# The opening of a two-block transformer kernel: VectorE takes over part of the weight split, and x's later quarters are transposed inside units

## The chip, the cores and the metric

One core of one Trainium2 chip runs one launch of the kernel. The metric is the device time in microseconds; less is better. Weights, activations and output are in DRAM in float32 at the start and at the end.

## The reference, cut to what matters

The kernel computes two transformer blocks on a sequence of 256 rows of 1024 columns. The change touches only the first step of the first block, the product of the normed input with `w_in`:

```python
def rms_norm(x, g):
    x32 = x.astype(jnp.float32)
    y = x32 * lax.rsqrt(jnp.mean(jnp.square(x32), axis=-1, keepdims=True) + RMS_EPS)
    return (y * g.astype(jnp.float32)).astype(x.dtype)

# first block: two attentions on slices of z, gated and merged, an MLP, a gated embedding
u = rms_norm(h, g_mix[i])          # (1, 256, 1024)
z = u @ w_in[i]                    # w_in: (1024, 4360)
q_a, k_a, v_a, q_b, k_b, v_b, f_b, gate_logits = jnp.split(z, SPLIT_POINTS, axis=-1)
```

The second block (sparse attention, retention, a gated MLP) follows with its own weights.

## The kernel before, in words

**Products in three parts.** TensorE multiplies in the type float32r, which keeps fewer bits than float32. So each operand is split: the upper half is its copy in float32r (`w_hi`, `xT_hi`), the lower half what is left (`w_lo`, `xT_lo`), and a product is the sum of upper x upper, upper x lower and lower x upper. ScalarE makes the upper halves with a copy, VectorE the lower ones with a subtraction.

**Units.** Weights come in units: two contraction tiles of 128 rows by 512 columns, 512 KB, one load on SP's queue into one of eight slots of `raw`; the split goes into one of four slots of `w_hi` and `w_lo`. A unit costs TensorE 12 products of 512 columns: two contraction tiles (`kk`), two tiles of 128 sequence rows (`t`), three parts. Units 0 to 3 make the first 512 columns of z (the queries), units 4 to 7 the next 512, and so on, until the last weights of the second block. The semaphores `hi_done`, `lo_done` and `units_used` count units split above, split below and used up. The root mean square is not applied in front: x times `g_mix` is multiplied, and the rows are scaled afterwards.

**The input.** x arrives in quarters of 256 columns (`load_x`, two loads of 128 KB each, semaphores `x_q0` to `x_q3`) into `h`. TensorE transposes them against the identity into banks of PSUM (`transposes`, four instructions a quarter, L1852). ScalarE copies a bank with `g_mix` as scale to `xT_hi` (`wide_hi`, L589: two operations, then one count of `wt_hi`), VectorE makes `xT_lo` from bank and copy (`wide_lo`, L1048, then one count of `wt_lo`). Unit `kp` of the first chunk needs the quarter `kp`. The first quarter is taken tile by tile (L639 on ScalarE, L1135 on VectorE).

**The order of the opening** is written out by hand, for each engine.
- SP (L424 to L433): first quarter of x; unit 0 in two loads of 256 KB (`first_in` and `landed[0]`); second quarter; unit 1 in one load; third quarter; unit 2; last quarter; units 3 to 7.
- GpSimd (L489): after a small constant it clears the padded arrays of keys and values, four instructions on Z, and then waits for the first norm.
- TensorE (L1892 to L1956): six products of ones by ones as filler (`ones_products`, L1890); transpose of `g_mix`; transposes of x's first quarter; two more fillers; unit 0's first contraction tile (six products, L1943, L1946, L1949); transposes of the second quarter; unit 0's second tile; transposes of the third quarter; unit 1 (L1920, L1924, L1927); transposes of the last quarter; units 2 and 3 (`unit_pair_lows_last`, L1734, L1743, L1746); then the usual units (`unit_pair`, L1709 to L1711).
- ScalarE (L634 to L660): `g_mix`; x's first tile (L639); the first tile of unit 0 (L643); x's second tile; unit 0's second tile (L646); the second quarter of x; unit 1 in two operations (L651); the third quarter of x; units 2 and 3 (`split_to`, L569); the last quarter; unit 4; sums of squares of x (L605); unit 5; and so on.
- VectorE (L1126 to L1151): four clearings and constants, `ones` the last; lower halves of x and unit 0, tile by tile (L1135, L1138); second quarter; unit 1 (L1145); third quarter; units 2 and 3 (L1032); last quarter; units 4 and 5.

An engine works through its instructions in order, and a wait holds all that stand behind it.

Of the kernel before, what the change touches and what calls it, by code (L numbers as in the profile page):

```python
# [7 lines left out]
P = 128  # L8
F32 = mybir.dt.float32
F32R = mybir.dt.float32r  # L10
BF16 = mybir.dt.bfloat16
ALU = mybir.AluOpType
# [47 lines left out]
def constants():  # L60
# [33 lines left out]
    "ident_in": "identity", "first_in": "first contraction tile of the first unit", "first_hi": "ACT: its upper half", "first_lo": "DVE: its lower half", "consts_in": "the other constants", "x_q0": "x, first quarter of the columns", "x_q1": "x, second quarter", "x_q2": "x, third quarter of its columns", "x_q3": "x, the last",  # L94
    "second_hi": "ACT: upper half of the second unit's first contraction tile", "second_lo": "DVE: its lower half",
# [76 lines left out]
def build(nc, x, p, g_mix, w_in, b_forget, swa_sinks, w_br_swa, w_br_fox, w_mix_out, g_mlp, w_ff1, w_ff2,  # L172
# [87 lines left out]
    with ExitStack() as ctx:  # L260
# [5 lines left out]
        def sem(name):  # L266
            return sems[name]
# [144 lines left out]
        def _(sp):  # L412
# [15 lines left out]
            load(1)  # L428
# [129 lines left out]
        def _(act):  # L558
# [78 lines left out]
            for kk, (bank, x_half) in enumerate(((2, sem("x_hi")), (6, sem("wt_hi")))):  # L637
                act.wait_ge((sem("x_T"), sem("wt_done"))[kk], 1)
                nc.scalar.activation(xT_hi[:, kk, :], B[:, bank, 0:SEQ], ACT.Copy,  # L639
                                     scale=vec[:, V_GMIX + kk:V_GMIX + kk + 1]).then_inc(x_half, 1)  # L640
                if kk == 0:
                    act.wait_ge(sem("first_in"), 16)
                    nc.scalar.activation(w_hi[:, 0, 0, :], raw[:, 0, 0, :], ACT.Copy).then_inc(sem("first_hi"), 1)  # L643
# [6 lines left out]
            for kk, upper_half in enumerate((sem("second_hi"), hi_done)):  # L650
                nc.scalar.activation(w_hi[:, 1, kk, :], raw[:, st.slot[1], kk, :], ACT.Copy).then_inc(upper_half, 1)  # L651
# [365 lines left out]
        def _(dve):  # L1017
# [107 lines left out]

            nc.vector.memset(one_row[:, :], 0.0).then_inc(sem("zeros"), 1)  # L1126
# [3 lines left out]
            nc.vector.memset(ones, 1.0).then_inc(sem("ones"), 1)  # L1130
            dve.wait_ge(sem("vec_done"), 1)
            for kk, (x_upper, x_lower, upper_half, lower_half) in enumerate(((sem("x_hi"), sem("x_lo"), sem("first_hi"), sem("first_lo")),
                                                                             (sem("wt_hi"), sem("wt_lo"), hi_done, lo_done))):
                dve.wait_ge(x_upper, 1)
                nc.vector.scalar_tensor_tensor(xT_lo[:, kk, :], B[:, (2, 6)[kk], 0:SEQ], vec[:, V_GMIX + kk:V_GMIX + kk + 1],  # L1135
                                               xT_hi[:, kk, :].bitcast(F32), ALU.mult, ALU.subtract).then_inc(x_lower, 1)
                dve.wait_ge(upper_half, 1)
                nc.vector.tensor_tensor(w_lo[:, 0, kk, :], raw[:, 0, kk, :], w_hi[:, 0, kk, :].bitcast(F32),  # L1138
                                        ALU.subtract).then_inc(lower_half, 1)
            wt[0] = 1  # L1140
            done[0] = 1
            wide_lo((3,), xT_hi, xT_lo, 2, V_GMIX)
            for kk, (upper_half, lower_half) in enumerate(((sem("second_hi"), sem("second_lo")), (hi_done, lo_done))):
                dve.wait_ge(upper_half, 1 + kk)
                nc.vector.tensor_tensor(w_lo[:, 1, kk, :], raw[:, st.slot[1], kk, :], w_hi[:, 1, kk, :].bitcast(F32),  # L1145
                                        ALU.subtract).then_inc(lower_half, 1)
# [559 lines left out]
        def _(pe):  # L1706
# [20 lines left out]

            def unit_pair_lows_last(u, xh, xl, kt0, banks, last):
# [3 lines left out]
                for kk in range(2):  # L1732
                    for t in range(TILES):
                        nc.tensor.matmul(B[:, banks[t], :], xh[:, kt0 + kk, rows_of(t)], w_hi[:, s, kk, :], start=False, stop=False)  # L1734
                for lows in ("weights", "rows") if last else ("rows", "weights"):
# [150 lines left out]

            def ones_products(n):
# [12 lines left out]
            ones_products(2)  # L1900
            for c in range(5):
                banks = (2 * (c % 2), 2 * (c % 2) + 1)
                for kp in range(4):
# [12 lines left out]
                    if u == 1:  # L1916
                        for kk, (upper_half, lower_half) in enumerate(((sem("second_hi"), sem("second_lo")), (hi_done, lo_done))):
                            pe.wait_ge(upper_half, 1 + kk)
                            for t in range(TILES):
                                nc.tensor.matmul(B[:, banks[t], :], xT_hi[:, 2 + kk, rows_of(t)], w_hi[:, 1, kk, :], start=False, stop=False)  # L1920
                            if kk == 0:
                                pe.wait_ge(sem("wt_lo"), 2)
                            for t in range(TILES):
                                nc.tensor.matmul(B[:, banks[t], :], xT_lo[:, 2 + kk, rows_of(t)], w_hi[:, 1, kk, :], start=False, stop=False)  # L1924
                            pe.wait_ge(lower_half, 1 + kk)
                            for t in range(TILES):
                                m = nc.tensor.matmul(B[:, banks[t], :], xT_hi[:, 2 + kk, rows_of(t)], w_lo[:, 1, kk, :], start=False, stop=False)  # L1927
                        m.then_inc(units_used, 1)
# [8 lines left out]
                    else:  # L1937
                        for kk, (x_upper, upper_half, x_lower, lower_half) in enumerate((
                                (sem("x_hi"), sem("first_hi"), sem("x_lo"), sem("first_lo")), (sem("wt_hi"), hi_done, sem("wt_lo"), lo_done))):
                            pe.wait_ge(x_upper, 1)  # L1940
                            pe.wait_ge(upper_half, 1)
                            for t in range(TILES):
                                nc.tensor.matmul(B[:, banks[t], :], xT_hi[:, kk, rows_of(t)], w_hi[:, 0, kk, :], start=kk == 0, stop=False)  # L1943
                            pe.wait_ge(x_lower, 1)
                            for t in range(TILES):
                                nc.tensor.matmul(B[:, banks[t], :], xT_lo[:, kk, rows_of(t)], w_hi[:, 0, kk, :], start=False, stop=False)  # L1946
                            pe.wait_ge(lower_half, 1)
                            for t in range(TILES):
                                m = nc.tensor.matmul(B[:, banks[t], :], xT_hi[:, kk, rows_of(t)], w_lo[:, 0, kk, :], start=False, stop=False)  # L1949
                            if kk == 0:  # L1950
                                pe.wait_ge(sem("x_q1"), 32)
                                transposes((3,), lambda t, k: h[:, t, (2 + k) * P:(3 + k) * P], "wt_done")
                        m.then_inc(units_used, 1)
                    if u < 2:
                        pe.wait_ge(sem(("x_q2", "x_q3")[u]), 32)
                        transposes((4 + u,), lambda t, k: h[:, t, (4 + 2 * u + k) * P:(5 + 2 * u + k) * P], "wt_done")  # L1956
# [388 lines left out]
```

## Time and profile before

| | |
|---|---|
| Runs without a profile | 824.35, 824.30, 824.13 us; median 824.3 |
| The profiled execution's own time | 823.81 us |
| Its span, first to last instruction | 822.1 us |
| Mean granted TensorE clock in the span | 0.998 |
| Busy: TensorE, its weight loads, VectorE, ScalarE, GpSimd | 812.8, 677.7, 629.3, 462.9, 61.9 us |
| Read from DRAM over the span | 170.42 MB |

The profile is of one execution. Its times in the rows count from the first instruction of the span; an engine's busy time is the union of its instructions' spans, and matmuls overlap, so that the end of one in the timeline lies behind the start of the next. The chain of waits is followed back from the last instruction, at each step to what released it or to the instruction before it on its engine; its pieces don't overlap, and a piece of TensorE there ends where its last product ends. In the timeline consecutive instructions of one kind are one row: start, us from the first start to the last end, engine, line, operation, out<-in, shapes, count, and in brackets the idle time before it with what ended it. PE is TensorE, PEld its weight loads, DVE VectorE, ACT ScalarE, POOL GpSimd.

### The profile page before, as it was taken

How to read it: one execution, taken by the hardware profiler on the slowest of the kernel's cores; microseconds unless marked ns; L12 is line 12 of the kernel's file. 1: busy time of each engine (PE TensorE's matmuls, PEld its weight loads, DVE VectorE, ACT ScalarE, POOL GpSimd, SP SyncE). 2: the span in 40 equal slices, each digit the busy share in tenths (PEclk: the TensorE clock that was granted, in tenths of full speed). 3: DMA queues.
4: the chain of work that ended last, by engine and by line, in shares of the span. 5: the costliest groups of instructions: out<-in, count | busy, mean ns of one | idle time of the engine just before them, and what ended most of it. 6: DMA issues, size and time to landing. Idle time of an engine off the chain costs nothing.

```text
span 822.1 us, 12294 instructions
## 1 busy us (share of the span) xinstructions
PE 812.8 (99%) x4272; PEld 677.7 (82%) x4272; DVE 629.3 (77%) x965; ACT 462.9 (56%) x751; POOL 61.9 (8%) x89
## 2 busy tenths in 40 slices
PE   9999999999999999999999999999999999999996
PEld 7897777898888888877978877888888888888885
DVE  5567777687888898878878997456796877677776
ACT  6657765466555555568544466446346654455444
POOL 2100000110011110301510000010000000000000
PEclk9999999999999999999999999999999999999999
DMA  9867435779999999543965574555544666655641
GB/s 302 275 198 237 136 126 182 251 273 405 346 335 340 319 323 336 191 120 106 272 213 143 164 218 137 171 154 153 180 154 128 201 189 209 196 178 172 209 130 52
DMA packets 89213, 173.15 MB, mean 211 GB/s; under 512 B 6553, under 2 KB 37001, under 8 KB 89041
## 3 DMA queue, kind: packets, MB, share of 16 engines
q1 hardware_dynamic: 83008, 142.56, 54.2%
q0 software_dynamic: 6000, 29.93, 10.5%
q8 instruction: 27, 0.44, 0.2%
q14 instruction: 18, 0.14, 0.0%
q10 hardware_dynamic: 160, 0.07, 0.0%
HBM read 170.42 MB, written 1.06 MB: 209 GB/s over the span
## 4 chain that ended last, share of the span: by engine, by line
PE 95%; DVE 2%; issue 1%; ACT 1%; POOLq 0%; POOL 0%; ACTq 0%; DVEq 0%
PE B L1709 19%; PE B L1711 19%; PE B L1710 19%; PE B L1772 15%; PE B L1775 8%; PE B L1852 2%; PE B L1787 2%; PE B L1882 2%; PE B L1860 1%; PE B L1873 1%; PE B L2126 1%; PE B L1790 1%; DVE w_lo L1032 1%; PE B L1818 0%; PE B L1809 0%
## 5 line engine op out<-in xcount | busy, mean ns | idle before, releaser
L1032 DVE TENSOR_TENSOR w_lo<-raw,w_hi 128x1024 fp32r<-128x1024 f32 (+3 forms) x154 | 184.8, 1209 | 49.4 <-ACT w_hi L569 47.9
L1709 PE MATMUL B<-w_hi,xT 128*128 128x512 f32 (+3 forms) x536 | 209.5, 391 | 0.0
L569 ACT ACTIVATE w_hi<-raw 128x1024 fp32r<-128x1024 f32 (+3 forms) x154 | 157.5, 1030 | 88.6 <-PE B L1711 74.6
L1711 PE MATMUL B<-w_hi,xT 128*128 128x512 f32 (+3 forms) x536 | 204.5, 381 | 0.0
L1710 PE MATMUL B<-w_lo,xT 128*128 128x512 f32 (+3 forms) x536 | 204.1, 381 | 0.0
L1709 PEld LDWEIGHTS B<-w_hi,xT 128*128 128x128 f32 x536 | 100.8, 188 | 20.7 <-issue 2.2
L1711 PEld LDWEIGHTS B<-w_hi,xT 128*128 128x128 f32 x536 | 100.7, 188 | 19.8
L1710 PEld LDWEIGHTS B<-w_lo,xT 128*128 128x128 f32 x536 | 100.9, 188 | 17.4
L1772 PE MATMUL B<-xT,w_hi 128*128 128x512 f32 x320 | 100.5, 395 | 0.0
L982 ACT ACTIVATE w_hi<-raw 128x1024 fp32r<-128x1024 f32 x60 | 62.2, 1055 | 42.5 <-PE B L1775 30.9
L1302 DVE TENSOR_TENSOR w_lo<-raw,w_hi 128x1024 fp32r<-128x1024 f32 x56 | 67.2, 1221 | 21.7 <-ACT w_hi L787 20.8
L1709 PE MATMUL B<-w_hi,sT 128*128 128x512 f32 (+1 forms) x201 | 78.9, 393 | 0.0
L1638 DVE TENSOR_TENSOR w_lo<-raw,w_hi 128x1024 fp32r<-128x1024 f32 x60 | 72.5, 1220 | 7.6 <-ACT w_hi L982 7.6
L1710 PE MATMUL B<-w_lo,sT 128*128 128x512 f32 (+1 forms) x201 | 77.9, 388 | 0.0
L1711 PE MATMUL B<-w_hi,sT 128*128 128x512 f32 (+1 forms) x201 | 77.9, 387 | 0.0
L787 ACT ACTIVATE w_hi<-raw 128x1024 fp32r<-128x1024 f32 x56 | 57.5, 1053 | 35.0 <-PE B L1775 30.6
L1775 PEld LDWEIGHTS B<-xT,w_lo 128*128 128x128 f32 x320 | 60.1, 188 | 14.1
L1772 PE MATMUL B<-sT,w_hi 128*128 128x512 f32 x224 | 70.3, 395 | 0.0
L1775 PE MATMUL B<-xT,w_lo 128*128 128x256 f32 x320 | 62.9, 278 | 0.0
L1310 DVE SCALAR_TENSOR_TENSOR Z<-Z,small 128x1536 f32<-128x1536 f32 x28 | 50.8, 1813 | 0.0
L1775 PEld LDWEIGHTS B<-sT,w_lo 128*128 128x128 f32 x224 | 42.1, 188 | 9.9
L1772 PEld LDWEIGHTS B<-xT,w_hi 128*128 128x128 f32 x320 | 49.4, 189 | 0.9 <-DVE Z L1624 0.2
(270 smaller groups left out, 1071.4 us busy)
## 6 DMA issues: line engine op xcount, KB each, us to landing
raw<-in_w_in_dram SPq DMA_DIRECT2D x79, 512.0 KB, 3.9
raw<-in_w_ff_dram SPq DMA_DIRECT2D x64, 512.0 KB, 7.4
Z<-in_w_ada_dram POOLq DMA_DIRECT2D x32, 768.0 KB, 7.6
raw<-in_w_ffn_gate_dram SPq DMA_DIRECT2D x44, 256.0 KB, 3.4
raw<-in_w_ffn_up_dram SPq DMA_DIRECT2D x44, 256.0 KB, 4.1
raw<-in_w_ffn_down_dram SPq DMA_DIRECT2D x20, 512.0 KB, 4.3
raw<-in_w_mix_out_dram SPq DMA_DIRECT2D x8, 512.0 KB, 3.7
raw<-in_w_ple_gate_dram SPq DMA_DIRECT2D x8, 512.0 KB, 4.3
```

The source lines that it names most:

```text
L569: nc.scalar.activation(w_hi[:, u % SPLIT, :, 0:n], raw[:, st.slot[u], :, 0:n], ACT.Copy).then_inc(hi_done, 1)
L787: nc.scalar.activation(w_hi[:, u % SPLIT, :, :], raw[:, st.slot[u], :, :], ACT.Copy).then_inc(hi_done, 1)
L982: nc.scalar.activation(w_hi[:, u % SPLIT, :, :], raw[:, st.slot[u], :, :], ACT.Copy).then_inc(hi_done, 1)
L1032: nc.vector.tensor_tensor(w_lo[:, u % SPLIT, :, 0:n], raw[:, st.slot[u], :, 0:n], w_hi[:, u % SPLIT, :, 0:n].bitcast(F32), ALU.subtract).t ...
L1302: nc.vector.tensor_tensor(w_lo[:, u % SPLIT, :, :], raw[:, st.slot[u], :, :], w_hi[:, u % SPLIT, :, :].bitcast(F32), ALU.subtract).then_in ...
L1310: nc.vector.scalar_tensor_tensor(ada_acc[:, 1536 * q:1536 * (q + 1)], ada_raw[:, q, :], silu_now, ada_acc[:, 1536 * q:1536 * (q + 1)], ALU ...
L1638: nc.vector.tensor_tensor(w_lo[:, u % SPLIT, :, :], raw[:, st.slot[u], :, :], w_hi[:, u % SPLIT, :, :].bitcast(F32), ALU.subtract).then_in ...
L1709: nc.tensor.matmul(bank, xh, wh, start=start, stop=False)
L1710: nc.tensor.matmul(bank, xh, wl, start=False, stop=False)
L1711: return nc.tensor.matmul(bank, xl, wh, start=False, stop=stop)
L1772: nc.tensor.matmul(B[:, i, :], w_hi[:, s, kk, cols], x2[:, kt0 + kk, :, :].rearrange("p e n -> p (e n)"), start=first and kk == 0, stop=False)
L1775: m = nc.tensor.matmul(B[:, i, SEQ:2 * SEQ], w_lo[:, s, kk, cols], x2[:, kt0 + kk, 0, :], start=False, stop=last and kk == 1)
```

## The change

The change has five parts, all in the opening.
- SP loads unit 1 in two halves, `second_in` and `landed[1]`.
- VectorE makes the upper half of unit 0's first contraction tile and of unit 1's first contraction tile, with a copy (`tensor_copy`), and each lower half right behind it; ScalarE no longer does. VectorE sets `ones` first of its constants, and takes the lower halves of x's first two tiles before the lower half of unit 0's second tile.
- TensorE computes one filler product instead of two before unit 0.
- In units 0 and 1 the products stand in another order, the weights' lower half before x's lower half (`products`, two products a call).
- The transposes of x's second quarter stand before unit 0's last pair of products, those of the third quarter inside unit 1 behind its sixth product, those of the last quarter inside unit 2 behind its fourth. Before, they stood behind unit 0's sixth product, behind unit 0 and behind unit 1.

```diff
@@ sync @@
-            load(1)
+            for kk, name in enumerate((sem("second_in"), landed[1])):
+                sp.dma_start(raw[:, st.slot[1], kk, :], w_in1[(2 + kk) * P:(3 + kk) * P, 0:512]).then_inc(name, 16)
@@ scalar @@
-                if kk == 0:
-                    act.wait_ge(sem("first_in"), 16)
-                    nc.scalar.activation(w_hi[:, 0, 0, :], raw[:, 0, 0, :], ACT.Copy).then_inc(sem("first_hi"), 1)
...
-            for kk, upper_half in enumerate((sem("second_hi"), hi_done)):
-                nc.scalar.activation(w_hi[:, 1, kk, :], raw[:, st.slot[1], kk, :], ACT.Copy).then_inc(upper_half, 1)
+            nc.scalar.activation(w_hi[:, 1, 1, :], raw[:, st.slot[1], 1, :], ACT.Copy).then_inc(hi_done, 1)
@@ vector @@
+            nc.vector.memset(ones, 1.0).then_inc(sem("ones"), 1)
             nc.vector.memset(one_row[:, :], 0.0).then_inc(sem("zeros"), 1)
...
-            nc.vector.memset(ones, 1.0).then_inc(sem("ones"), 1)
+            def opening_lo(slot, kk, upper_half, count, lower_half):
+                dve.wait_ge(upper_half, count)
+                nc.vector.tensor_tensor(w_lo[:, slot, kk, :], raw[:, st.slot[slot], kk, :], w_hi[:, slot, kk, :].bitcast(F32),
+                                        ALU.subtract).then_inc(lower_half, 1)
+
+            dve.wait_ge(sem("first_in"), 16)
+            nc.vector.tensor_copy(w_hi[:, 0, 0, :], raw[:, 0, 0, :]).then_inc(sem("first_hi"), 1)
+            opening_lo(0, 0, sem("first_hi"), 1, sem("first_lo"))
             dve.wait_ge(sem("vec_done"), 1)
-            for kk, (x_upper, x_lower, upper_half, lower_half) in enumerate(((sem("x_hi"), sem("x_lo"), sem("first_hi"), sem("first_lo")),
-                                                                             (sem("wt_hi"), sem("wt_lo"), hi_done, lo_done))):
+            for kk, (x_upper, x_lower) in enumerate(((sem("x_hi"), sem("x_lo")), (sem("wt_hi"), sem("wt_lo")))):
                 dve.wait_ge(x_upper, 1)
                 nc.vector.scalar_tensor_tensor(xT_lo[:, kk, :], B[:, (2, 6)[kk], 0:SEQ], vec[:, V_GMIX + kk:V_GMIX + kk + 1],
                                                xT_hi[:, kk, :].bitcast(F32), ALU.mult, ALU.subtract).then_inc(x_lower, 1)
-                dve.wait_ge(upper_half, 1)
-                nc.vector.tensor_tensor(w_lo[:, 0, kk, :], raw[:, 0, kk, :], w_hi[:, 0, kk, :].bitcast(F32),
-                                        ALU.subtract).then_inc(lower_half, 1)
             wt[0] = 1
-            done[0] = 1
+            opening_lo(0, 1, hi_done, 1, lo_done)
+            dve.wait_ge(sem("second_in"), 16)
+            nc.vector.tensor_copy(w_hi[:, 1, 0, :], raw[:, st.slot[1], 0, :]).then_inc(sem("second_hi"), 1)
+            opening_lo(1, 0, sem("second_hi"), 1, sem("second_lo"))
             wide_lo((3,), xT_hi, xT_lo, 2, V_GMIX)
...
+            opening_lo(1, 1, hi_done, 2, lo_done)
@@ tensor @@
+            def opening_transposes(name, bank, k0):
+                pe.wait_ge(sem(name), 32)
+                transposes((bank,), lambda t, k: h[:, t, (k0 + k) * P:(k0 + k + 1) * P], "wt_done")
+
             def unit_pair_lows_last(u, xh, xl, kt0, banks, last):
...
+                if u == 2:
+                    opening_transposes("x_q3", 5, 6)
...
+            def products(banks, rows, k, w, slot, kk, first=False):
+                for t in range(TILES):
+                    m = nc.tensor.matmul(B[:, banks[t], :], rows[:, k, rows_of(t)], w[:, slot, kk, :], start=first, stop=False)
+                return m
...
-            ones_products(2)
+            ones_products(1)
...
                     if u == 1:
+                        pe.wait_ge(sem("second_hi"), 1)
+                        products(banks, xT_hi, 2, w_hi, 1, 0)
+                        pe.wait_ge(sem("second_lo"), 1)
+                        products(banks, xT_hi, 2, w_lo, 1, 0)
+                        pe.wait_ge(hi_done, 2)
+                        products(banks, xT_hi, 3, w_hi, 1, 1)
+                        opening_transposes("x_q2", 4, 4)
+                        pe.wait_ge(sem("wt_lo"), 2)
+                        products(banks, xT_lo, 2, w_hi, 1, 0)
+                        products(banks, xT_lo, 3, w_hi, 1, 1)
+                        pe.wait_ge(lo_done, 2)
+                        products(banks, xT_hi, 3, w_lo, 1, 1).then_inc(units_used, 1)
...
                     else:
+                        pe.wait_ge(sem("x_hi"), 1)
+                        pe.wait_ge(sem("first_hi"), 1)
+                        products(banks, xT_hi, 0, w_hi, 0, 0, True)
+                        pe.wait_ge(sem("first_lo"), 1)
+                        products(banks, xT_hi, 0, w_lo, 0, 0)
+                        pe.wait_ge(sem("x_lo"), 1)
+                        products(banks, xT_lo, 0, w_hi, 0, 0)
+                        pe.wait_ge(sem("wt_hi"), 1)
+                        pe.wait_ge(hi_done, 1)
+                        products(banks, xT_hi, 1, w_hi, 0, 1)
+                        pe.wait_ge(sem("wt_lo"), 1)
+                        products(banks, xT_lo, 1, w_hi, 0, 1)
+                        opening_transposes("x_q1", 3, 2)
+                        pe.wait_ge(lo_done, 1)
+                        products(banks, xT_hi, 1, w_lo, 0, 1).then_inc(units_used, 1)
```

The loops that these lines of TensorE replace are in the printed functions above. ScalarE's order is otherwise as it was: the third quarter's copies stand before the split of units 2 and 3.

## Rows read from the trace of the kernel before

**Rows 1.** The page, busy us of each engine (share of the span) and instructions.
```profile
PE 812.8 (99%) x4272; PEld 677.7 (82%) x4272; DVE 629.3 (77%) x965; ACT 462.9 (56%) x751; POOL 61.9 (8%) x89
```

**Rows 2.** Waits of TensorE over the whole span: us in total, times, longest.
```profile
PE B L1890 <- DVE ones_r L1130: 1.4, 1, 1.4
```

**Rows 3.** The chain of waits, 0 to 20 us: start, us, what.
```profile
1.44 2.93 PE B L1890 x6
...
5.72 0.85 PE B L1890 x2
6.57 0.66 PE B L1943 x2
...
8.15 0.44 PE B L1852 x4
...
9.98 0.44 PE B L1852 x4
...
13.20 0.44 PE B L1852 x4
13.64 0.93 PE B L1734 x4
...
16.40 0.91 PE B L1734 x4
...
18.21 0.91 PE B L1743 x4
```

**Rows 4.** The timeline around the first product: start, us, engine, line, operation.
```profile
5.39 0.47 ACT L639 ACTIVATE xT<-B,vec 128x256 fp32r<-128x256 f32 x1 [0.61 <-PE B L1852]
...
5.77 0.62 ACT L643 ACTIVATE w_hi<-raw 128x512 fp32r<-128x512 f32 x1
...
6.42 0.69 DVE L1138 TENSOR_TENSOR w_lo<-raw,w_hi 128x512 fp32r<-128x512 f32 x1
...
6.53 0.70 PE L1943 MATMUL B<-w_hi,xT 128*128 128x512 f32 x2
```

**Rows 5.** DMA issues at 1.81 and 3.70 us: xcount, KB each, us to landing.
```profile
raw<-in_w_in_dram SPq DMA_DIRECT2D x1, 256.0 KB, 3.5
...
raw<-in_w_in_dram SPq DMA_DIRECT2D x1, 512.0 KB, 5.3
```

**Rows 6.** VectorE groups by line and shape: busy us, mean ns, idle before.
```profile
L1385 DVE CAST xT<-Z 128x256 fp32r<-128x256 f32 x16 | 4.6, 289 | 2.6 <-ACT Z L860 2.6
L1111 DVE TENSOR_SCALAR Z<-Z,small 128x256 f32<-128x256 f32 x24 | 8.3, 348 | 0.0
L1111 DVE TENSOR_SCALAR Z<-Z,small 128x128 f32<-128x128 f32 x24 | 6.9, 287 | 0.8
```

**Rows 7.** The timeline of GpSimd at 5.3 us.
```profile
4.13 1.92 POOL L489 MEMSET Z<- 128x2176 f32 x1
```

**Rows 8.** The timeline of VectorE and GpSimd where they overlap, 179.5 and 380 us.
```profile
179.85 1.02 DVE L1269 TENSOR_SCALAR Z<-Z,small 128x1536 f32<-128x1536 f32 x1
...
180.02 1.42 POOL L484 TENSOR_TENSOR small<-small 128x2 f32<-128x2 f32 x1 [24.44 <-DVE small L1063]
...
380.21 0.54 POOL L530 TENSOR_TENSOR small<-small 128x1 f32<-128x1 f32 x1
...
380.26 0.29 DVE L1371 TENSOR_SCALAR rstd_id<-cst,small 128x128 f32<-128x128 f32 x1 [0.40 <-POOL small L484]
```

**Rows 9.** The timeline, from transposed quarters of x to ScalarE's copies.
```profile
7.99 0.60 PE L1852 MATMUL B<-cst,h 128*128 128x128 f32 x4
...
8.63 0.84 ACT L589 ACTIVATE xT<-B,vec 128x256 fp32r<-128x256 f32 x2 [1.36 <-PE B L1852]
...
9.36 1.15 ACT L651 ACTIVATE w_hi<-raw 128x512 fp32r<-128x512 f32 x2
...
11.19 1.06 ACT L569 ACTIVATE w_hi<-raw 128x1024 fp32r<-128x1024 f32 x1
```

**Rows 10.** The timeline, VectorE's split of the sixth unit.
```profile
18.63 1.22 DVE L1032 TENSOR_TENSOR w_lo<-raw,w_hi 128x1024 fp32r<-128x1024 f32 x1 [0.84 <-ACT w_hi L569]
```

More of the change, by code:

```diff
@@ L92 @@
 SIGNALS = {
-    "ident_in": "identity", "first_in": "first contraction tile of the first unit", "first_hi": "ACT: its upper half", "first_lo": "DVE: its lower half", "consts_in": "the other constants", "x_q0": "x, first quarter of the columns", "x_q1": "x, second quarter", "x_q2": "x, third quarter of its columns", "x_q3": "x, the last",
-    "second_hi": "ACT: upper half of the second unit's first contraction tile", "second_lo": "DVE: its lower half",
+    "ident_in": "identity", "first_in": "first contraction tile of the first unit", "first_hi": "DVE: its upper half", "first_lo": "DVE: its lower half", "consts_in": "the other constants", "x_q0": "x, first quarter of the columns", "x_q1": "x, second quarter", "x_q2": "x, third quarter of its columns", "x_q3": "x, the last",
+    "second_in": "first contraction tile of the second unit", "second_hi": "DVE: upper half of the second unit's first contraction tile", "second_lo": "DVE: its lower half",
     "x_T": "PE: x's first contraction tile transposed", "x_hi": "ACT: upper half of x's first contraction tile", "x_lo": "DVE: its lower half",
@@ L1136, in _ @@
                                                xT_hi[:, kk, :].bitcast(F32), ALU.mult, ALU.subtract).then_inc(x_lower, 1)
-                dve.wait_ge(upper_half, 1)
-                nc.vector.tensor_tensor(w_lo[:, 0, kk, :], raw[:, 0, kk, :], w_hi[:, 0, kk, :].bitcast(F32),
-                                        ALU.subtract).then_inc(lower_half, 1)
             wt[0] = 1
-            done[0] = 1
+            opening_lo(0, 1, hi_done, 1, lo_done)
+            dve.wait_ge(sem("second_in"), 16)
+            nc.vector.tensor_copy(w_hi[:, 1, 0, :], raw[:, st.slot[1], 0, :]).then_inc(sem("second_hi"), 1)
+            opening_lo(1, 0, sem("second_hi"), 1, sem("second_lo"))
             wide_lo((3,), xT_hi, xT_lo, 2, V_GMIX)
[L1143 to L1146, printed above, removed]
+            opening_lo(1, 1, hi_done, 2, lo_done)
             done[0] = 2
@@ L1916, in _ @@
                     if u == 1:
[L1917 to L1928, printed above, removed]
+                        pe.wait_ge(sem("second_hi"), 1)
[10 more added lines that the diff above has]
+                        products(banks, xT_hi, 3, w_lo, 1, 1).then_inc(units_used, 1)
                     elif u in (2, 3):
@@ L1937, in _ @@
                     else:
[L1938 to L1956, printed above, removed]
+                        pe.wait_ge(sem("x_hi"), 1)
+                        pe.wait_ge(sem("first_hi"), 1)
+                        products(banks, xT_hi, 0, w_hi, 0, 0, True)
+                        pe.wait_ge(sem("first_lo"), 1)
```

## The prediction

> **What bounds the kernel now.** I read the page first: TensorE is busy for 812.8 of 822.1 us [rows 1], so only time in which it stands still, or filler that it computes, can be won. The view of waits then asks what TensorE waits for: one entry, 1.4 us before its very first instruction [rows 2]. Everything else stands in the chain of waits, in order of time, which in the opening runs over TensorE alone [rows 3]. The reader is to see that its pieces touch: filler ends at 6.57 us, the first pair of products at 7.23, the transposes of x's second quarter at 8.59, of the third at 10.42, unit 1 at 13.20, the transposes of the last quarter at 13.64, then unit 2 to 16.40 and unit 3 to 19.12. Four products take 0.91 us, 0.23 each; four transposes 0.44. From 6.57 us on there is no gap to remove. What the change can win is the start, and what it can lose is this density.
>
> A second thing is in the same rows: the two filler products took 0.43 us each (0.85 for two), those after 6.57 us 0.23. These are the two levels of the clock, 1.2 and 2.4 GHz; TensorE had been at work since 1.44 us when it rose, near 6.4 us.
>
> **What sets the start.** The timeline around the first product [rows 4]: ScalarE makes x's upper half until 5.39 + 0.47 = 5.86, then the weights' upper half until 5.77 + 0.62 = 6.39, and the first product starts at 6.53, 0.14 after that. The pair ends at 6.53 + 0.70 = 7.23. The change gives that weight half to VectorE. Its weights land at 1.81 + 3.5 = 5.3 us [rows 5].
>
> **Cost of the cast on VectorE.** The trace has casts of 256 columns, both sides in SBUF, at 289 ns; TENSOR_SCALAR takes 287 ns for 128 columns and 348 for 256 [rows 6], so 0.48 ns a column. 512 columns are then 289 + 256 x 0.48 = 412 ns, taken as 0.42 us. Bounds: 0.29 (256 columns) and 0.69 (a VectorE subtraction of 512, rows 4). Nothing in its way, the cast ends at 5.3 + 0.1 + 0.42 = 5.8, x's half at 5.86 decides, and the first product starts at 6.0: 0.5 us won. The clock takes part of it back, since until about 6.4 a product takes 0.43: the second starts at about 6.47 and the pair ends at 6.86, 0.37 before today's 7.23.
>
> **The port.** Something is in its way. GpSimd clears 2176 columns from 4.13 to 6.05 us in one instruction [rows 7]. Where VectorE runs a fast one-input instruction, the trace shows GpSimd held: a TENSOR_SCALAR of 1536 columns runs 179.85 to 180.87, and GpSimd's little power operation of 180.02 takes 1.42 us instead of 0.54 [rows 8], so that it ends 0.57 after the other. So one keeps the other out for a whole instruction. Here the order is the reverse, GpSimd first. The nearest row for that, a TENSOR_SCALAR at 380.26 begun 0.05 us into a GpSimd operation, shows nothing (0.29 us, as in rows 6), but that operation touches one column and can hold little. Between a wait of 0 and one until 6.05 I take the latter: the clearing writes throughout its 1.92 us. The cast then ends at 6.05 + 0.42 = 6.47 and the first product starts at 6.61, 0.08 later than now.
> The Trainium skill, "SBUF — State Buffer", section "Who interferes with whom", has the rule: VectorE in a two-port mode (copy and cast among its operations) and GpSimd share a port pair, and whoever issues first holds it for the whole instruction. By that rule the sum is the +1.94 below, without it +1.23; the trace agrees for the order VectorE first, and no row shows the other.
>
> **Unit 0.** The subtraction follows the cast: 6.50 + 0.69 = 7.19 [rows 4], so the third product starts at 7.33 instead of 7.07 and its pair ends at 8.03. Three pairs follow (lower half of x, then the second tile's two): 3 x 0.46, to 9.41. Their inputs are in time: VectorE makes x's two lower halves from 7.19 on, at most 0.69 each as a bound, so by 7.88 and 8.57, wanted at 8.03 and 8.95; the second upper half of the weights comes no later than today, since ScalarE has one operation less in front. Then the transposes of x's second quarter, moved from behind six products to behind ten: 9.85. That x has landed by then, since they run at 7.99 today [rows 9]. Behind them unit 0 has one pair left, 0.46.
>
> **Gap 1.** Unit 1 needs the columns transposed just now. ScalarE starts 0.04 after the transposes (7.99 + 0.60 = 8.59, start 8.63), its two copies take 0.84 [rows 9], the product follows 0.14 after, and a pair that starts on an idle array takes 0.70: 9.85 + 0.04 + 0.84 + 0.14 + 0.70 = 11.57 for the end of unit 1's first pair. Unhindered it were 9.85 + 2 x 0.46 = 10.77: a gap of 0.80. Today the same copies lie behind the second half of unit 0 and the third quarter's transposes (8.59 to 10.42).
>
> **Gap 2.** Two more pairs, to 12.49, then the third quarter's transposes, to 12.93, and three pairs as cover (1.38). ScalarE's queue, though, is in order: its two copies for that quarter, and only behind them the split of unit 2. Today the split runs at 11.19 with 1.06 us, long before 13.64. In the new order it starts 0.04 + 0.73 (8.63 to 9.36) after the transposes and ends, 1.06 later, at 14.76; the first pair of unit 2 ends at 14.76 + 0.14 + 0.70 = 15.60 against 14.77 unhindered: a gap of 0.83. Then a pair (16.06), the last quarter's transposes, now inside unit 2 (16.50), and four pairs: unit 2 ends at 18.34. Today: 16.40. The sum is +1.94.
>
> **Afterwards.** Unit 3's rows are copied by 16.50 + 0.88 = 17.4, before 18.34: no third gap. VectorE finished unit 5's split at 18.63 + 1.22 = 19.85 [rows 10] and TensorE needs it at 19.12 + 2.73 = 21.85; it moves with the rest, so 2 us of cover stay. The work removed, one filler product, is worth nothing: it filled a wait. The earlier filler, at the front, neither. One more DMA issue on SP costs 0.47 us of its queue (1.81 to 3.70 us is four issues, rows 5); x's later quarters and unit 2 are wanted later than today by more than that. Unit 1 lands whole at 3.70 + 5.3 = 9.0 today [rows 5], its first half so no later; VectorE is busy with unit 0 until at most 8.57 + 0.69 = 9.26, cast and subtraction of the half take it to 10.37, and TensorE wants them at 10.9 and 11.57. That cast finds GpSimd done with its clearing [rows 7]. The rest of the program is dense and its loads are freed by TensorE's progress, so I pass the delay on in full.
>
> **Sum.** Against the profiled execution, 823.8 us with a span of 822.1: 825.8. The median of the runs is 824.3, 0.5 above: 824.3 + 1.94 = **826.2 us**. A measurement tells about 0.2%, 1.65 us, from no change, so the line lies at 825.95: close, and the port decides on which side.
>
> **Rivals.**
> - No port wait, chance 0.25. First pair at 6.86, four pairs to 8.70, transposes 9.14, then the same two gaps: unit 2 ends at 17.63, +1.23, 825.5. For it speaks the row at 380.26; against it the one at 180.02. If the port pushes the transposes out by over 0.42 us (I have 0.71), the total passes 1.65.
> - The clock rises late, 0.10. It rose near 6.4 us, with TensorE at work since 1.44 almost without pause. In the new kernel it stands still from about 5.8 to 6.6. If it stays low through unit 0, twelve products cost 0.20 more each, 2.4 us: 828.6. Against it: today's pauses around the little transposes (4.37 to 5.3) did no harm.
> - Not slower, 0.07: the gaps do not open, because x's copies are ready within the one pair that follows the transposes. The place is unit 1's first product; it decides at 0.46 us after the transposes. The price is then that of the start alone: -0.37 without the port's wait, 823.9; +0.34 with it (8.03 for today's 7.69), 824.6. Against it: 0.04 + 0.84 + 0.14 are 1.02, of rows without a wait in them.
>
> **How the numbers follow.** The forecast has 0.55, and within it 0.1 for gaps small enough to stay under 1.65; 0.03 is for what I don't see. Slower 0.56 = 0.45 + 0.10 for the late clock + 0.01; same 0.42 = 0.25 + 0.10 + 0.07; faster 0.02. The forecast alone is 825.8 to 826.8 (cast 0.29 to 0.69, 0.15 either way on each gap); the range 825.0 to 827.3 takes in the rival without a wait and leaves out the late clock and the start alone.
>
> **What would show it.** In the new profile: the cast's end, 6.5 (port) or 5.8; the first product at 6.6 or 6.0; two waits of TensorE, on ScalarE's copy of x before unit 1 and on ScalarE's split of unit 2, some 0.7 to 0.8 us each in the spacing of products; a spacing of 0.23 from 6.6 on; unit 2's end at 18.34 and everything behind it 2 us late. Wrong it is if unit 1's first product starts before 10.3 with port wait, if unit 2 starts without a pause, or if a later stage takes the delay back.

## The result and the profile after

The changed kernel takes **825.48 us** (median of 11 runs, 825.34 to 826.87) against 824.10 for the kernel before beside it (11 runs, 823.66 to 824.35): ratio 1.0020, 95% interval 1.0012 to 1.0027. By the medians that is 1.38 us or 0.17% slower: inside the range of the prediction (825.0 to 827.3), but near its fast end, below the 825.8 to 826.8 that it gave for its own mechanism, and just under the 0.2% that it called distinguishable. The profiled execution took 825.48 us with a span of 823.7; the one of before 823.81 with 822.1.

The page (busy us, share, instructions) shows that TensorE does the same work and that the span is 1.6 us longer:

```profile
span 823.7 us, 12293 instructions
...
PE 813.2 (99%) x4271; PEld 677.3 (82%) x4271; DVE 631.1 (77%) x967; ACT 462.3 (56%) x749; POOL 61.8 (7%) x89
```

Where before there was one wait of TensorE [rows 2], the view of waits now has four (us in total, times, longest):

```profile
PE B L1906 <- DVE ones_r L1123: 1.2, 1, 1.2
PE B L1742 <- ACT w_hi L570: 0.6, 1, 0.6
PE B L1900 <- DVE w_hi L1136: 0.6, 1, 0.6
PE B L1900 <- ACT xT L590: 0.5, 1, 0.5
```

The three new ones are the three places of the prediction: VectorE's cast in front of unit 0 (L1136), ScalarE's copy of x in front of unit 1 (L590), ScalarE's split in front of unit 2 (L570). The chain of waits (start, us, what) puts them in order; it left TensorE nowhere in this stretch before [rows 3]:

```profile
5.05 1.29 DVE w_hi L1136
...
6.47 2.73 PE B L1900 x10
9.20 0.45 PE B L1862 x4
...
9.68 0.85 ACT xT L590 x2
10.53 0.04 issue
10.57 1.65 PE B L1900 x6
12.22 0.45 PE B L1862 x4
...
12.70 0.84 ACT xT L590 x2
13.54 0.96 ACT w_hi L570
14.49 0.14 issue
14.63 1.16 PE B L1742 x4
15.79 0.44 PE B L1862 x4
...
18.06 0.91 PE B L1742 x4
```

The reader is to see: the cast until 6.33; ten products, then the second quarter's transposes until 9.65; TensorE released only after both copies of x (9.68 to 10.53); six products and the third quarter's transposes until 12.68; then not only the copies but, behind them in ScalarE's queue, the split of unit 2 (13.54 to 14.49); the last quarter's transposes inside unit 2. Unit 2 ends at 18.06, where it ended at 16.40 [rows 3]: +1.66. The whole profiled execution is 1.67 longer. Nothing after unit 2 gave any of it back, and nothing added to it. The 1.66 are made up of 0.12 up to the end of the second quarter's transposes (9.65, where ten products and four transposes ended at 9.53 before), 0.73 for the pause before unit 1 and 0.82 for the one before unit 2; these are differences of the rows, rounded.

The timeline around the start (start, us, engine, line, operation, shapes, count), to be held against [rows 4, 7]:

```profile
4.13 1.92 POOL L490 MEMSET Z<- 128x2176 f32 x1
...
5.05 1.27 DVE L1136 CAST w_hi<-raw 128x512 fp32r<-128x512 f32 x1 [3.66 <-DMA raw<-in_w_in_dram]
6.36 0.69 DVE L1132 TENSOR_TENSOR w_lo<-raw,w_hi 128x512 fp32r<-128x512 f32 x1
...
8.35 0.42 DVE L1146 CAST w_hi<-raw 128x512 fp32r<-128x512 f32 x1
...
7.11 0.73 PE L1900 MATMUL B<-w_lo,xT 128*128 128x512 f32 x2
...
10.57 0.73 PE L1900 MATMUL B<-w_hi,xT 128*128 128x512 f32 x2 [0.46 <-ACT xT L590]
```

The clearing runs from 4.13 to 6.05 as before. The cast begins at 5.05 and takes 1.27; its twin for unit 1, at 8.35 with GpSimd idle, takes 0.42.

In six of the variants below the clearing also stands whole before the cast. The chains of two of them (first the one with all transposes at their old places, then the one with the second quarter put back) show the cast beginning at other moments, as its weights land:

```profile
5.00 1.34 DVE w_hi L1136
```

```profile
5.25 1.08 DVE w_hi L1136
```

Both end at 6.33 or 6.34. In all seven profiles with the whole clearing the cast begins between 5.00 and 5.28 and ends at 6.32 to 6.34: its end is tied to the clearing's, not to its own start.

### The profile page after: what moved, and what is told of

The parts are those of the page before. It is cut to its first block, busy times and chain, and to the rows that moved or that the text cites. A ratio compares the mean times of both kernels' runs of the same rounds, so it can differ in the third digit from the quotient of the medians.

```text
span 823.7 us, 12293 instructions
## 1 busy us (share of the span) xinstructions
PE 813.2 (99%) x4271; PEld 677.3 (82%) x4271; DVE 631.1 (77%) x967; ACT 462.3 (56%) x749; POOL 61.8 (7%) x89
## 3 DMA queue, kind: packets, MB, share of 16 engines
HBM read 170.42 MB, written 1.06 MB: 208 GB/s over the span
## 4 chain that ended last, share of the span: by engine, by line
PE 97%; ACT 0%; DVE 0%; DMA 0%; issue 0%; SPq 0%; POOLq 0%; POOL 0%; ACTq 0%; DVEq 0%
PE B L1712 20%; PE B L1714 20%; PE B L1713 20%; PE B L1782 15%; PE B L1785 8%; PE B L1862 2%; PE B L1797 2%; PE B L1892 2%; PE B L1870 1%; PE B L1883 1%; PE B L2138 1%; PE B L1800 1%; PE B L1900 1%; PE B L1828 0%; PE B L1819 0%; PE B L1830 0%
## 5 line engine op out<-in xcount | busy, mean ns | idle before, releaser
L570 ACT ACTIVATE w_hi<-raw 128x1024 fp32r<-128x1024 f32 (+3 forms) x154 | 157.4, 1030 | 87.7 <-PE B L1714 74.7
```

The lines of the kernel that those rows point to most:

```text
L570: nc.scalar.activation(w_hi[:, u % SPLIT, :, 0:n], raw[:, st.slot[u], :, 0:n], ACT.Copy).then_inc(hi_done, 1)
```

## The experiments

Each kernel is the changed one with the edit shown, unless said otherwise, and was run 11 times (one of them 9), with the kernel before beside it. One thing must be known to read the times: many of the kernels fall into two groups of runs whose means lie 1.4 to 1.7 us apart, and the profiles show what differs (below, the clock). Where it matters the lower groups are compared; that leaves out how many runs fall into the upper one, which changes from kernel to kernel and can put the median there.

**The port set free.**

```diff
@@ gpsimd @@
+            pool.wait_ge(sem("first_hi"), 1)
             zero(vb_pad[:, :, :])
```

> The changed kernel, but GpSimd starts its last clearing only after VectorE's cast of the first weights. Theory (the cast of 1.28 us is 0.42 of work and 0.86 of waiting for GpSimd's clearing of 4.13 to 6.04): the cast takes 0.42 and ends by 5.6, x's upper half decides (5.64), TensorE's first product starts at 5.8 instead of 6.47, and with the lower clock taking some of it back the time falls by 0.4 to 0.65 us, 825.5 to about 824.9. Rival (this cast is slow by itself, on freshly landed data or in this type): the cast stays near 1.28 and the time stays at 825.5.

Measured: 824.87 us (824.61 to 825.22), five runs at 824.61 to 824.66. The cast, in the timeline, and two pieces of the chain of waits, from an execution of 825.20:

```profile
5.15 0.43 DVE L1137 CAST w_hi<-raw 128x512 fp32r<-128x512 f32 x1 [3.76 <-DMA raw<-in_w_in_dram]
```

```profile
5.80 3.21 PE B L1901 x10
...
14.43 1.16 PE B L1743 x4
```

The cast takes 0.43 us: the waiting for GpSimd's clearing is shown, the rival is out. TensorE starts on this execution at 5.8 (of ten products those at the front take 0.43 each: 3.21 us for ten against 2.73 in the changed kernel), so part of the 0.7 won goes to the clock. The pauses before units 1 and 2 are still there, and in this execution, one of the slower of the 11, unit 2 starts only 0.2 earlier (14.43 for 14.63). The five quickest runs are 0.8 below the 825.4 of the changed kernel's main group.

**The clearing cut in two.**

```diff
@@ gpsimd @@
-            zero(vb_pad[:, :, :])
+            nc.gpsimd.memset(vb_pad[:, 0, :], 0.0)
+            zero(vb_pad[:, 1, :])
```

> The changed kernel, but GpSimd clears the last array in two instructions of 1088 columns instead of one of 2176. Nobody waits for anybody new. Theory (the port is held for one instruction and no longer): the first half ends at about 5.1, VectorE's cast of 5.05 starts behind it and ends by 5.6, the second half is held up in its turn, TensorE starts at 5.8, and the runs whose clock rises early come to 824.65 as in the run with the port free. Rival (GpSimd keeps the port as long as it has clearings queued): the cast ends at 6.3 as in the changed kernel, 825.4.

Measured: 825.52 (824.48 to 827.22). The timeline of GpSimd and of VectorE:

```profile
4.12 1.00 POOL L496 MEMSET Z<- 128x1088 f32 x1
5.07 1.00 POOL L490 MEMSET Z<- 128x1088 f32 x1
...
5.12 1.24 DVE L1137 CAST w_hi<-raw 128x512 fp32r<-128x512 f32 x1 [3.73 <-DMA raw<-in_w_in_dram]
```

The profile doesn't separate the two theories. The second half began at 5.07, the cast at 5.12, 0.05 later, and it ended at 6.36, behind the end of that half (6.07). So a lead of 0.05 us was enough for GpSimd to keep the cast out to the end of its instruction; that it does so only for one instruction, and not for as long as clearings are queued, isn't shown, since this was the last one. The profile and the main group of runs (five at 825.46 to 825.54) came out as the rival said. For the theory speak two of the 11 runs, 824.48 and 824.61, the time of the kernel with the port free: that the cast was first in them is likely, but they carry no profile.

**ScalarE splits unit 2 first.**

```diff
@@ scalar @@
+            split_to(2)
             wide_hi((4,), xT_hi, 4, V_GMIX)
             split_to(3)
```

> The changed kernel, but ScalarE splits unit 2 before it copies x's third quarter. Theory (gap 2 comes from ScalarE's order): TensorE starts unit 2 at 13.9 instead of 14.63, -0.7 us, 824.8. Rival (unit 2's weights are what is late: they landed at 11.8): a pause before unit 2 stays, now released by the DMA, and less than 0.3 is won.

Measured: median 825.93, with four runs at 824.66 to 824.71, one at 825.00 and six at 825.93 to 826.44. The profiled execution (826.44) is of the upper group; its ScalarE timeline and its waits of TensorE show what the edit does:

```profile
11.44 0.84 ACT L590 ACTIVATE xT<-B,vec 128x256 fp32r<-128x256 f32 x2 [4.77 <-PE B L1863]
...
12.68 1.06 ACT L570 ACTIVATE w_hi<-raw 128x1024 fp32r<-128x1024 f32 x1
14.46 0.84 ACT L590 ACTIVATE xT<-B,vec 128x256 fp32r<-128x256 f32 x2 [0.72 <-PE B L1863]
```

```profile
PE B L1901 <- ACT xT L590: 0.5, 1, 0.5
PE B L1901 <- DVE w_hi L1137: 0.4, 1, 0.4
```

The split of unit 2 (12.68) now stands before the copies of the third quarter (14.46), and the wait for it is gone from the view. In this execution everything came over 1.5 us later, so it can't tell whether unit 2's weights would be late in the lower group; the times can: the four runs at 824.7 are 0.7 under the changed kernel's 825.4. Gap 2 came from the order on ScalarE, at the size expected. The median is still above the changed kernel's, since more runs fell into the upper group.

**The second quarter's transposes back behind the sixth product.**

```diff
@@ tensor @@
                         products(banks, xT_lo, 0, w_hi, 0, 0)
+                        opening_transposes("x_q1", 3, 2)
...
                         products(banks, xT_lo, 1, w_hi, 0, 1)
-                        opening_transposes("x_q1", 3, 2)
```

> The changed kernel, but x's second quarter is transposed behind unit 0's sixth product, as before the change. Theory (gap 1 comes from the place of these four transposes): no pause before unit 1, its first product at 10.0 instead of 10.57, and gap 2 keeps its size, so -0.55 us, 824.9. Rival (x's second quarter or unit 1 lands too late to use the earlier place): a pause before the transposes takes its place, and the time stays within 0.2 of 825.5.

Measured: 824.74, with six runs at 824.65 to 824.74 and five at 826.07 to 826.50. The chain of waits of the profiled execution (826.50, upper group):

```profile
6.47 2.90 PE B L1900 x6
9.37 0.85 PE B L1862 x4
10.22 3.09 PE B L1900 x12
13.31 0.45 PE B L1862 x4
...
15.71 1.16 PE B L1742 x4
```

Twelve products of units 0 and 1 follow each other without a pause between the units: gap 1 is gone, gap 2 (until 15.71) is not. That is seen at the slower product rate, which gives x's copies more cover, but the times agree: in the lower group 0.7 is won. Expected was 0.55, which counted only the later start of unit 1; the pair that starts behind the pause also takes 0.73 (10.57 to 11.30) instead of 0.46.

**All transposes at their old places.** The edit just shown, and:

```diff
@@ tensor @@
-                if u == 2:
-                    opening_transposes("x_q3", 5, 6)
...
-                        opening_transposes("x_q2", 4, 4)
...
+                    if u < 2:
+                        opening_transposes(("x_q2", "x_q3")[u], 4 + u, 4 + 2 * u)
```

> The changed kernel with all of x's transposes at their places of before; left of the change are VectorE's casts, unit 1 in two loads, one filler less and the order of the products. Theory: no pause before units 1 and 2; only the port's wait and the third product's wait for the subtraction are left, TensorE 0.15 behind the kernel before at the sixth product and at unit 3, so 824.05 to 824.3 for runs whose clock rises early. Rival (the extra load or the order of the products costs something by itself): over 824.6 in these runs.

Measured: median 825.24, but four runs at 823.90 to 824.00 and seven at 825.17 to 825.76. In the waits of TensorE in the profiled execution (825.65, upper group), beside the one before its first instruction, this is all:

```profile
PE B L1898 <- DVE w_hi L1136: 0.7, 1, 0.7
```

Only the cast's wait is left. In the lower group the time is 823.95, 1.45 under the changed kernel, and about that of the kernel before: the casts, the extra load and the new order of the products together cost next to nothing here (0.1 less than expected). The moved transposes cost nearly all of the slowdown of the lower group, and the two gaps taken away one by one (0.7 each) add up to it. The upper group, though, is now most of the runs, and the median is 1.2 above the kernel before.

**The filler, and the clock.** One filler more, two more, none:

```diff
@@ tensor @@
-            ones_products(1)
+            ones_products(2)
```

> The changed kernel with two filler products in front of unit 0, as before the change, instead of one; TensorE waits there until 6.33 anyhow. The runs so far fall in two groups, 1.4 to 1.6 us apart, and in the profiles of the slower group the clock rises at 10.7 or 10.8 us instead of 5.8. Theory (the standstill before unit 0 decides how often it rises late): the time of the faster group stays at 825.4, and 0 or 1 run in 11 is in the slower group. Rival (it is independent of the filler): 2 to 6 of 11.

> The changed kernel with three filler products in front of unit 0, so that TensorE works until about 6.45, as long as it waits for the cast. Theory (the standstill in front of unit 0 lets the clock rise late): none of 11 runs in the slower group, as in the kernel before, where no run of 64 lay 1.4 us above the rest but one; the time stays at 825.4 to 825.6. Rival (something else in the new opening does it): 2 or more of 11 at 826.8 to 827.2.

> The changed kernel with no filler product in front of unit 0. Theory (the standstill decides): most of the 11 runs, 7 or more, are in the slower group, and the median is about 826.9. Rival (independent of the filler): 2 to 6 of 11, and the median mostly at 825.5.

Measured: with two, 825.51, eight runs at 825.42 to 825.54 and three at 826.99 to 827.11. With three, 825.45, and none of 11 runs above 825.92. With none, 826.94: four of nine at 825.36 to 825.49, five at 826.94 to 827.27. The changed kernel with its one filler: nine at 825.34 to 825.54, two at 826.82 and 826.87. None of the edits moves the lower group; what differs is how many runs lie in the upper. And in the other direction, on the kernel before:

```diff
@@ tensor, the kernel before @@
-            ones_products(2)
+            ones_products(1)
```

> The kernel before with one filler product instead of two in front of unit 0; its first product still waits for ScalarE until 6.5. Theory (the standstill): 2 to 6 of 11 runs come out 1.2 to 1.7 us above the rest, at about 825.2 to 825.6, the rest at 823.6 to 824.4. Rival: no such run, 824.0 as before.

Measured: 823.77, nine runs at 823.57 to 824.30 and two at 825.40 and 825.73. The profiled one took 825.73; its chain of waits (pieces of two products, the first also with the start):

```profile
6.43 1.19 PE B L1943 x2
7.62 0.85 PE B L1946 x2
...
10.18 0.85 PE B L1943 x2
11.04 0.55 PE B L1946 x2
11.58 0.46 PE B L1949 x2
```

A pair of products takes 0.85 us, 0.43 each, until about 11.1, and 0.46 from then on: by the duration of the products the clock stayed at 1.2 GHz for two thirds of unit 0, where in the kernel before it had risen by 6.57 [rows 3]. The profile of the kernel with the second quarter put back (826.50) shows the same above, 0.85 us for its first four transposes where they take 0.44 otherwise, and the chain of the profiled execution without filler (827.06) has ten slow products in front of the second quarter's transposes, against 2.73 us in the changed kernel:

```profile
6.47 4.39 PE B L1900 x10
```

The level is read from durations alone: the granted clock that the profiles give is 1.00 in every stretch between 4.5 and 12 us, in both groups.

Taken alone, 0 of 11 with three fillers against 2 of 11 with one proves little, and so does 2 of 11 for the kernel before with one filler, against 2 of 97 with its own two. But the other kernels can be sorted in the same way, each against kernels run beside it on the same chip:

- Without a standstill, the port free (the first experiment and the version with the third quarter inside unit 1, below): 1 of 22 runs in an upper group. Beside them, with the cast's wait (ScalarE's split first, the second quarter back): 11 of 22.
- With the cast's wait (the clearing cut, two fillers, none, all old places): 19 of 42. Beside them, the kernel before: 0 of 31.
- Without a standstill or with one of 0.2 us (three fillers, and the two versions below in their last runs): 0 of 33.

So that a standstill in front of unit 0 goes with the upper group is shown. Its size is not: two fillers leave a wait of 0.3 us for the cast by the view of waits (one leaves 0.6, none 1.0, three no such entry), and still gave 3 of 11, where 0 or 1 was expected, and without filler it was 5 of 9, where 7 were. With one filler it was 2 of 11 in the changed kernel, but 6 of 11 with ScalarE's split moved, an edit that touches nothing before about 11 us, and 4, 5 and 7 of 11 in the other variants with one filler and the cast's wait. So 11 runs don't tell 0.3 from 1.0 us, and what length of standstill at which moment matters stays open.

**Versions with the port free and fewer pauses.** The kernel with all old places, and GpSimd's wait from the first experiment:

> The changed kernel with the port free and all of x's transposes at their places of before. Theory: first product at 5.75, but the third quarter of x lands at 9.2 to 9.6, after TensorE could take it, at 9.0, and unit 2 at 11.8 plus its split, 13.0, against 12.9 that TensorE could start it: of 0.75 won at the start at most 0.4 is left at unit 3, 823.3 to 823.7 in the faster runs. Rival (nothing in the way of the early start): 823.0 or less.

Measured: 823.79 (823.20 to 824.65) against 823.81 for the kernel before beside it. The chain of waits of an execution of 823.2:

```profile
5.75 1.83 PE B L1899 x6
...
13.04 0.92 PE B L1743 x4
```

Unit 2 starts at 13.04, 0.6 before the 13.64 of [rows 3]: x's third quarter and unit 2 were in time, and of the 0.75 won at the start more was left than the 0.4 expected. The time, 823.20, lies between the theory's 823.3 to 823.7 and the rival's 823.0. The median still shows nothing of it: the runs spread over 1.45 us. That TensorE, starting at 5.75, does more or less of unit 0 at the lower clock from run to run would explain this, but it isn't shown, since only one of the runs has a profile.

The other one has the third quarter inside unit 1 and the rest at the old places:

```diff
@@ gpsimd @@
+            pool.wait_ge(sem("first_hi"), 1)
             zero(vb_pad[:, :, :])
@@ tensor @@
-                if u == 2:
-                    opening_transposes("x_q3", 5, 6)
...
                         products(banks, xT_lo, 0, w_hi, 0, 0)
+                        opening_transposes("x_q1", 3, 2)
...
-                        opening_transposes("x_q1", 3, 2)
...
+                    if u == 1:
+                        opening_transposes("x_q3", 5, 6)
```

> The changed kernel with the port free (as in the first of these runs), x's second quarter transposed behind unit 0's sixth product and the last quarter behind unit 1, the third still inside unit 1. Theory: first product at 5.8, unit 1 from 9.1, and unit 2 bound by its own landing (11.8) and split (1.06), so from about 13.1; unit 2 without transposes inside. Unit 3 then starts at about 15.95 against 16.24 in the kernel before: 823.8, 0.3 faster than before. Rival (the landing of x's third or last quarter takes the place of the pauses removed): no faster than before, 824.1 to 824.5.

> The combination of the first call once more, on another chip or at another time: 823.5 to 823.8 for its median and 0.1 to 0.4 us less than the kernel before beside it, if the first reading was no accident; otherwise no difference or slower.

Measured: 823.71 against 823.90 (ratio 1.0000, interval 0.9991 to 1.0009), and again 823.53 against 823.81 (0.9996, 0.9987 to 1.0005). The chain of waits of the first:

```profile
5.80 1.76 PE B L1899 x6
7.57 0.44 PE B L1861 x4
8.01 2.76 PE B L1899 x12
10.77 0.44 PE B L1861 x4
11.20 1.40 PE B L1899 x6
12.60 0.61 PE B L1861 x4
13.21 1.13 PE B L1743 x4
```

TensorE is alone in the chain again, from 5.80 on; unit 2 starts at 13.2, where 13.1 was expected. The reason given was not quite the right one: ScalarE's timeline has the split of unit 2 at 11.97, straight behind its copies of the third quarter, so that its queue and not the landing sets the 13.2. In the profile of the repetition (823.90) the same two steps are back in the chain, and unit 2 starts at 13.53: with the third quarter's transposes inside unit 1 there is next to no cover to spare. Both medians are 0.2 to 0.3 us under the kernel before and 1.8 to 2.0 under the changed one. The latter is clear; the former is smaller than its interval, twice with the same sign, and I don't call it faster.

## Why the prediction was right, point by point

- **The port.** Predicted: the cast held until 6.05, end 6.47, first product 6.61. Measured: end 6.33, first product 6.47. The wait is real and shown by the run with the port free, the duration of the cast too (0.42 and 0.43 for 0.42; the sum had stretched casts of 256 columns). The size was off by 0.14: behind the clearing only 0.28 us of the cast was left, not its full 0.42. What the wait is worth was mis-sized as well: the rival's sum put it at 0.71, the profile with the port free has unit 2 only 0.2 earlier, and the quickest runs there gain 0.8.
- **Unit 0.** Predicted: third product 7.33, transposes of the second quarter done 9.85. Measured 7.11 and 9.65. Of the 0.20, 0.14 is the cast's. The product followed 0.06 after the subtraction's end (7.05), not 0.14; the 0.14 is right only where the weights' upper half itself is waited for, as here at 6.47 and 14.63.
- **Gap 1.** Predicted 0.80; from the transposes' end to the first pair's end 1.72, measured 1.65 (9.65 to 11.30), again by the shorter release: 0.04 (10.53 to 10.57).
- **Gap 2.** Predicted 3.13 from the third quarter's transposes to the end of unit 2's first four products (12.93 to 16.06); measured 3.12 (12.67 to 15.79). The end of unit 2: predicted +1.94, measured +1.66. Nearly all of the difference lies in front of gap 1 (0.12 for 0.32); the gaps were 0.73 for 0.80 and 0.82 for 0.83.
- **Passed on in full.** Right: 1.66 at unit 2, 1.67 in the time.
- **The number.** 826.2 was predicted, 825.48 measured, 0.7 less: 0.28 by the sum above, 0.2 because the kernel before had a median of 824.10 beside it and not 824.3, and 0.3 because the medians differ by less than the profiled executions (next point). It is luck that 825.48 is to 0.1 the time of the rival without a port wait, 825.5, whose mechanism the profile excludes: from the time alone the two could not have been told apart.
- **Median.** 1.38 where the profiled executions differ by 1.67. The kernel before was profiled near the lower end of its runs. A likely reason for its spread of 0.7 us against 0.2 in nine of the 11 of the changed kernel: its first product starts near the moment at which the clock rises, while the changed kernel stands still then and loses nothing by a rise somewhat later. That fits the run with the port free, which starts earlier and spreads over 0.6, but it was not tested by itself. It is also luck that only 2 of the 11 runs lay in the upper group: in the variants with the same filler and the same wait it was 4 to 7 of 11, and with 6 the median would have been near 826.8.
- **The rivals.** No port wait: out. Not slower: out, both gaps opened as summed. The late clock: there, in 2 of 11 runs of this kernel, too few to set its median, but in 22 of 44 runs of the four variants with the same filler and the same wait, so 0.10 was too low for a single run; its price was 1.4 us instead of 2.4, as the two runs show. The term of that sum was mis-sized: it took all twelve products of unit 0 at 0.20 more each, from 6.6 on. In the profile without filler the ten products up to the transposes took 1.66 more, and unit 2 starts 1.66 later (16.29 for 14.63): the last pair was quick again, and the wait for the subtraction before the third product, some 0.2 us, was hidden behind the slower products (both worked out from the rows, as estimates).
- **The chances.** Slower by over 0.2% had 0.56, same 0.42. By the medians it came out at 0.17%, so on the side with the smaller chance. The too long releases and the cast's tail (0.28 us) alone would have left 1.66, right at the line of 1.65; the rest is the 0.3 between medians and profiled executions. With a line that near to the sum the chances were right to be nearly even, but the 0.42 was made up mostly of the two rivals that are out, and only 0.10 of small gaps.

## What to carry to other kernels

Where TensorE has no gap, an operation moved to a later place on it is not free even if the total stays the same: ask how many products stand between it and its first reader, and lay the whole way (here two copies, 0.84 us, and, in ScalarE's queue, a split of 1.06 behind them) beside them. Before giving an operation to VectorE, look at what GpSimd runs at that moment: here a copy between SBUF tiles waited for a clearing to its end. And in these kernels filler that ended before the first product went with 1.5 us more in some of the runs, so look at all runs and not at their median alone.

## What the runs showed of the hardware

- GpSimd's clearing keeps VectorE's cast out for the rest of its instruction: 1.27 us instead of 0.42, and 1.24 behind a clearing that had begun 0.05 us earlier. That is shown for clearings. In the row of before VectorE, begun 0.05 us into a GpSimd operation of 0.54 us on one column, was not held (0.29 us, [rows 8]), so a GpSimd operation need not keep VectorE out for its whole length. The Trainium skill, "SBUF — State Buffer", section "Who interferes with whom", says that the first to issue holds the shared pair for its whole instruction; by that rule, the runs with a clearing agree, for the order GpSimd first, and the row just named doesn't.
- A cast from float32 to float32r, 128x512 in SBUF, takes 0.42 us on VectorE, where ScalarE's copy took 0.62 [rows 4].
- The clock's rise, read from the durations of the products, came in these kernels anywhere from before 6.5 us (the changed kernel's first pair took 0.70, as that of the kernel before did at 2.4 GHz) to about 11.1, though TensorE began at 1.2 to 1.4 in all. With a standstill of 0.3 to 1.0 us in front of unit 0 it came only near the end of unit 0 in some executions of the same program, and those took 1.4 to 1.7 us longer; without one this was rare (1 of 22, 0 of 33, 2 of 97).
